# Strassen's seven products for half of a down projection, in a one-core transformer block in split float32

## What is computed

```python
m = rmsnorm(h, norm_mlp_g[l])
h = h + jnp.square(jax.nn.relu(m @ w_up[l])) @ w_down[l]      # w_up 2048 x 8192, w_down 8192 x 2048
return rmsnorm(h[:, CHUNK:CHUNK + S], final_norm_g)
```

## Time and profile before

| what | us |
|---|---|
| median of three runs (1141.16 to 1141.45) | 1141.17 |
| the profiled execution | 1139.69 |
| its span, first to last instruction | 1137.8 |
| TensorE busy | 1118.9 |
| VectorE busy | 714.9 |
| ScalarE busy | 605.3 |
| start of the first up stage, by the timeline | 415.8 |
| last matmul done | 1130.3 |

### The profile page before, as it was taken

One profiled execution on the slowest core, in us unless ns is written; L12 is line 12 of the kernel. 1 busy time (PEld: TensorE's weight loads), 2 busy tenths in 40 slices (PEclk: granted clock), 3 DMA queues, 4 the chain that ended last, 5 costly groups with the idle time before them and its releaser, 6 DMA issues.

```text
span 1137.8 us, 16740 instructions
## 1 busy us (share of the span) xinstructions
PE 1118.9 (98%) x6220; PEld 969.4 (85%) x6220; DVE 714.9 (63%) x986; ACT 605.3 (53%) x919; POOL 66.4 (6%) x78
## 2 busy tenths in 40 slices
PE   7999999999999999999999999999999999999997
PEld 7899999999878888888888888888888888888885
DVE  6986877777786666666664444446666665454453
ACT  8665666666665555555553333334555554344343
POOL 0001110111123320000000000000000000000000
PEclk9999999999999999999999999999999999999999
DMA  9544544334355545555555555555555555555541
GB/s 365 203 155 146 182 143 154 141 131 155 130 190 206 214 167 198 190 190 191 190 186 185 185 187 188 194 198 188 192 185 184 184 184 185 190 191 193 198 154 74
DMA packets 29573, 206.64 MB, mean 182 GB/s; under 512 B 3408, under 2 KB 3664, under 8 KB 5200
## 3 DMA queue, kind: packets, MB, share of 16 engines
q1 hardware_dynamic: 29232, 205.59, 50.8%
q10 hardware_dynamic: 288, 0.31, 0.1%
HBM read 203.79 MB, written 2.10 MB: 181 GB/s over the span
## 4 chain that ended last, share of the span: by engine, by line
PE 96%; ACT 1%; DVE 1%; DMA 1%; issue 0%; SPq 0%; POOL 0%; POOLq 0%; DVEq 0%
PE acc L329 58%; PE ps_qn L329 9%; PE ps_qr L329 9%; PE ps_v L329 8%; PE ps_kn L329 8%; PE ps_x L329 2%; DMA x_in<-x_all 1%; ACT hi L704 0%; PE ps_y L329 0%; ACT xs L742 0%; PE ps_qn L623 0%; PE ps_kn L494 0%; PE ps_y L522 0%; PE ps_qr L623 0%; SPq L271 0%
## 5 line engine op out<-in xcount | busy, mean ns | idle before, releaser
L1025 DVE TENSOR_TENSOR lo<-raw,hi 128x1024 fp32r<-128x1024 f32 (+1 forms) x379 | 462.6, 1221 | 290.7 <-ACT hi L704 286.6
L329 PE MATMUL acc<-xs,hi 128*128 128x512 f32 (+1 forms) x1952 | 586.3, 363 | 0.0
L704 ACT ACTIVATE hi<-raw 128x1024 fp32r<-128x1024 f32 (+1 forms) x379 | 397.8, 1050 | 293.2 <-PE ps_v L329 106.2
L329 PE MATMUL acc<-xs,lo 128*128 128x256 f32 (+1 forms) x1648 | 454.8, 284 | 7.2 <-DVE xs L1042 6.6
L329 PEld LDWEIGHTS acc<-xs,hi 128*128 128x128 f32 x1952 | 345.5, 189 | 51.9
L329 PEld LDWEIGHTS acc<-xs,lo 128*128 128x128 f32 x1648 | 311.7, 189 | 14.3 <-issue 6.6
L704 ACT ACTIVATE half_b<-acc 128x256 f32<-128x256 f32 x100 | 38.5, 385 | 155.0 <-PE acc L329 155.0
L329 PE MATMUL ps_v<-hi,hid 128*128 128x512 f32 x256 | 101.4, 396 | 0.0
L329 PE MATMUL ps_kn<-hi,hid 128*128 128x512 f32 x256 | 100.7, 393 | 0.0
L329 PE MATMUL ps_qr<-hi,hid 128*128 128x512 f32 x256 | 100.3, 396 | 0.0
L329 PE MATMUL ps_qn<-hi,hid 128*128 128x512 f32 x256 | 99.6, 393 | 0.0
(11 more groups left out here) (236 smaller groups left out, 942.1 us busy)
## 6 DMA issues: line engine op xcount, KB each, us to landing
raw<-w_up SPq DMA_DIRECT2D x64, 1024.0 KB, 4.7
raw<-w_down SPq DMA_DIRECT2D x64, 1024.0 KB, 4.7
raw<-w_in SPq DMA_DIRECT2D x42, 1024.0 KB, 4.7
raw<-w_o SPq DMA_DIRECT2D x16, 1024.0 KB, 4.8
h_res<-x_frames SPq DMA_DIRECT2D x1, 2048.0 KB, 7.6
x_in<-x_all SPq DMA_DIRECT2D x3, 544.0 KB, 7.5
consts<-consts_in SPq DMA_DIRECT2D x1, 1218.5 KB, 10.4
raw<-w_in SPq DMA_DIRECT2D x2, 512.0 KB, 8.6
```

Of the source, the lines that this page charges most:

```text
L329: return pe.matmul(o, l, m, start=start, stop=stop)
L704: return act.activation(o, i, ACT.Copy)
L1025: return dve.tensor_tensor(o, a, b, op)
```

## The change

**Seven products.** Half of the down projection (by hidden tiles) is computed in blocks of two by two: two hidden tiles a and b of 128 (a "pair"), two frame tiles, two column groups of 512. Eight block products become Strassen's seven (p1 to p7, in Winograd's form), each still of three matmuls of 512 columns. Each product sums over the pairs in its own bank: `p1 ps_qr, p2 ps_kn, p3 ps_v, p4 acc[1], p5 ps_x, p6 ps_qn, p7 acc[0]`; an eighth bank, `p8 ps_y`, takes one of the plain sums.

**Four segments.** The hidden columns go in 4 segments of 16 tiles: 16 up chunks, then 16 down chunks. Tiles 0 to 7 of a segment stay plain, tiles 8 to 15 form 4 pairs. Down chunks come in two sets of eight, one for each half of the output columns (a "mix"): pair 0, first 0, pair 1, second 0, pair 2, first 1, pair 3, second 1, where first and second are plain chunks of the left and the right column group, added into p2 and p4, and into p3 and p8. In the last segment the second set is 8 plain chunks with banks of their own. So there are 7 mixes and 28 pair chunks.

**On chip.** For a pair VectorE makes three mixed weights from raw (`t_31`, 1024 wide; `t_2`, 512, written over a quarter of raw; `t_4`, 512), ScalarE rounds them (`t_hi`, 1536 wide), VectorE makes `t_lo` (1536). In the up stage VectorE makes four mixed activations of 128 x 128 (`mixed_acts`), ScalarE rounds them (512 wide), VectorE makes their lo. After the last pair chunk of a mix ScalarE copies the product banks to SBUF (`read_out`: six, and p3 after the last plain chunk), VectorE adds p8 to `res`. The rest (`merge`, seven additions of 512 or 1024 elements per mix) is made by VectorE in the first eight up chunks of the next segment, or in the quad chunks at the end.

**Room.** Three raw buffers in the MLP in place of four (the fourth holds t_hi and a kept product); `gfin` is loaded in the last segment, into `xs`. The MLP's loops are written out.

```diff
+MIX = [("pair", 0), ("first", 0), ("pair", 1), ("second", 0), ("pair", 2), ("first", 1), ("pair", 3), ("second", 1)]
+TAIL_MIX = [("quad", q) for _ in range(2) for q in range(SEG // PER_CHUNK)]
...
+READ_ORDER = ("p2", "p6", "p1", "p7", "p5", "p4", "p3")
+STEPS = 7
...
             def load(src, c, more=0):
                 if c >= RAWS:
-                    sp.wait_ge(sem["lo_ready"], 2 * (c - RAWS) + 2 + 2 * more)
-                sp.dma_start(raw[c % RAWS][:], src).then_inc(raw_landed[c % RAWS], 16)
+                    before = c - (RAWS_MLP if c >= C_MLP + RAWS_MLP else RAWS)
+                    sp.wait_ge(sem["lo_ready"], 2 * before + 2 + 2 * more)
+                    if before in PAIR_OF:
+                        sp.wait_ge(sem["t_4"], PAIR_OF[before] + 1)
+                sp.dma_start(raw[raw_of(c)][:], src).then_inc(raw_landed[raw_of(c)], 16)
...
+            def product(o, x, w, first, last):
+
+                mm(o[:], x[0], w[0], first, False)
+                mm(o[:], x[0], w[1], False, False)
+                return mm(o[:], x[1], w[0], False, last)
...
+                pe.wait_ge(sem["lo_ready"], 2 * c + 1)
+                pe.wait_ge(sem["up_lo"], SEG * s + b + 1)
+                pe.wait_ge(sem["s_lo"], PAIRS * s + i + 1)
+                if first and mix:
+                    pe.wait_ge(sem["p_read"], STEPS * mix - 1)
+                product(prod["p2"], act_of(s, b, 0), unit(c, 0), first, last)
+                if first and mix:
+                    pe.wait_ge(sem["p_read"], STEPS * mix)
+                product(prod["p3"], mixed_act(3), unit(c, 1), first, False).then_inc(sem["chunk_used"], 1)
+                pe.wait_ge(sem["lo_ready"], 2 * c + 2)
+                product(prod["p6"], mixed_act(1), unit(c, 2), first, last)
+                product(prod["p1"], act_of(s, a, 0), unit(c, 3), first, last).then_inc(sem["chunk_used"], 1)
+                pe.wait_ge(sem["t_lo"], p + 1)
+                if first and g == 0:
+                    pe.wait_ge(sem["acc_read"], B_MLP + SEG * (s + 1))
+                product(prod["p7"], mixed_act(2), mixed_weight(0), first, last)
+                product(prod["p5"], mixed_act(0), mixed_weight(1), first, last)
+                product(prod["p4"], act_of(s, b, 1), mixed_weight(2), first, last).then_inc(sem["t_used"], 1)
...
                 act.wait_ge(sem["chunk_used"], 2 * (c - 2) + part + 1 + 2 * more)
+                if c in PAIR_OF and part == 1:
+                    act.wait_ge(sem["t_2"], PAIR_OF[c] + 1)
                 copy(halves(hi, c, part), raw_half(c, part)).then_inc(sem["hi_ready"], 1)
+                if c in PAIR_OF and part == 1:
+                    act.wait_ge(sem["t_4"], PAIR_OF[c] + 1)
+                    act.wait_ge(sem["t_used"], PAIR_OF[c])
+                    copy(t_hi[:], t_raw[:]).then_inc(sem["t_hi"], 1)
...
+                    split_hi(c + 2, 0)
+                    if d == 0:
+                        sums_hi(PAIRS * s + PAIRS - 1)
+                    if kind == "second" and n == QUADS - 1:
+                        act.wait_ge(sem["chunk_used"], 2 * c + 2)
+                        read_out(s, g, READ_ORDER[6:])
+                    split_hi(c + 2, 1)
+                    if kind == "pair" and n == PAIRS - 1:
+                        if s:
+                            act.wait_ge(sem["merged"], 2 * STEPS * s)
+                        act.wait_ge(sem["chunk_used"], 2 * c + 2)
+                        read_out(s, g, READ_ORDER[:3])
+                        act.wait_ge(sem["t_used"], PAIR_OF[c] + 1)
+                        read_out(s, g, READ_ORDER[3:6])
...
+                if p is not None and part == 0:
+                    dve.wait_ge(raw_landed[raw_of(c)], 16 * landings(c))
+                    if p:
+                        dve.wait_ge(sem["t_lo"], p)
+                    tt(t_of[:, 0:2, :], u[:, 1:3, :], u[:, 2:4, :], ALU.subtract).then_inc(sem["t_31"], 1)
+                    dve.wait_ge(sem["t_31"], p + 1)
+                    tt(u[:, 2, :], u[:, 1, :], t_of[:, 1, :], ALU.subtract).then_inc(sem["t_2"], 1)
+                if p is not None and part == 1:
+                    dve.wait_ge(sem["t_2"], p + 1)
+                    tt(t_of[:, 2, :], u[:, 0, :], u[:, 2, :], ALU.subtract).then_inc(sem["t_4"], 1)
                 dve.wait_ge(sem["hi_ready"], 2 * c + part + 1 + 2 * more)
                 tt(halves(lo, c, part), raw_half(c, part), halves(hi, c, part).bitcast(F32),
                    ALU.subtract).then_inc(sem["lo_ready"], 1)
+                if p is not None and part == 1:
+                    dve.wait_ge(sem["t_hi"], p + 1)
+                    tt(t_lo[:], t_raw[:], t_hi[:].bitcast(F32), ALU.subtract).then_inc(sem["t_lo"], 1)
...
+                    if j > PLAIN and j % 2:
+                        mixed_acts(PAIRS * s + pair)
+                    if s and j < PLAIN:
+                        for _ in range((2, 2, 1, 2, 2, 1, 2, 2)[j]):
+                            merge(merges)
+                            merges += 1
```

More of the change, by code:

```diff
@@ L304, in _ @@
                     load(w_o[4 * i + j], C_WO + j, 4 * i)
[L305 to L315, removed]
+            for s in range(SEGS):
+                c0 = C_MLP + s * C_SEG
+                for j in range(SEG):
+                    load(w_up[SEG * s + j], c0 + j)
+                for d in range(2 * HALF_D):
+                    load(w_down[2 * HALF_D * s + d], c0 + SEG + d)
+                    if s == SEGS - 1 and d == HALF_D:
+                        sp.wait_ge(sem["chunk_used"], 2 * (c0 + SEG))
+                        sp.dma_start(gfin[:], gfin_in).then_inc(sem["gfin"], 16)
             sp.wait_ge(sem["fin_act"], 1)
@@ new lines, in quad_chunk @@
+            def quad_chunk(s, c, q, banks, firsts, lasts):
+                for j in range(PER_CHUNK):
+                    if j % 2 == 0:
+                        pe.wait_ge(sem["lo_ready"], 2 * c + j // 2 + 1)
+                    for t in range(TILES):
+                        m = product(banks[t], act_of(s, PER_CHUNK * q + j, t), unit(c, j), firsts[t] and j == 0,
+                                    lasts[t] and j == PER_CHUNK - 1)
+                    if j % 2 == 1:
+                        m.then_inc(sem["chunk_used"], 1)
@@ L636, in m_parts @@
+            for s in range(SEGS):
+                c0, b0 = C_MLP + s * C_SEG, B_MLP + s * SEG
                 def m_parts(k):
                     pe.wait_ge(sem["m_lo"], k + 1)
[L639 to L665, removed]
@@ L682, in _ @@
[L682 to L698 removed]
+                if s:
+                    pe.wait_ge(sem["p_read"], STEPS * 2 * s - 1)
@@ new lines, in _ @@
+                for j in range(SEG):
+                    wide(c0 + j, b0 + j, x_wide, x_hi, ready=m_parts if s == 0 and j == 0 else None)
+                    if s == 0 and j == 0:
+                        turn(KT - 1)
+                        pe.wait_ge(sem["h_ss"], KT)
+                        mm(ps_x[:, 0:FRAMES], ones, sum_sq[:]).then_inc(sem["h_ss_ps"], 1)
+                cd = c0 + SEG
+                if s == 0:
+                    pe.wait_ge(sem["ht"], TILES * KT // 4)
+                    pe.wait_ge(sem["h_sd"], 1)
@@ new lines, in _ @@
+            for s in range(SEGS):
+                c0, b0, w0 = C_MLP + s * C_SEG, B_MLP + s * SEG, W_MLP + s * SEG
+                for j in range(SEG):
+                    n = SEG * s + j
+                    pair = (j - PLAIN) // 2
+                    acc_of[0] = acc[(b0 + j) % 2]
+                    split_hi(c0 + j + 2, 0)
+                    if j > PLAIN and j % 2 == 0:
+                        sums_hi(PAIRS * s + pair - 1)
+                    b_copy(c0 + j, w0 + j)
+                    split_hi(c0 + j + 2, 1)
+                    if s == 0 and j == 0:
@@ L1415, in up @@
+            merges = 0
+            for s in range(SEGS):
+                c0, b0, w0 = C_MLP + s * C_SEG, B_MLP + s * SEG, W_MLP + s * SEG
+                for j in range(SEG):
+                    n = SEG * s + j
+                    pair = (j - PLAIN) // 2
+                    split_lo(c0 + j + 2, 0)
+                    sum_ab(z[:], b0 + j, w0 + j).then_inc(sem["acc_read"], 1)
+                    if s == 0 and j == 0:
                         dve.wait_ge(sem["h_sd"], 1)
```

375 lines of the change are left out of this document (258 added, 117 removed).

## The result

| | before | after |
|---|---|---|
| median (runs) | 1141.16 us (1139.66 to 1141.45, 4) | 1121.87 us (1120.81 to 1123.17, 4) |
| the profiled execution | 1139.69 | 1123.17 |
| its span | 1137.8 | 1121.4 |

The ratio is 0.9836, 95% interval 0.9824 to 0.9848: 17.3 to 20.1 us faster. The forecast was 1127.5, the range 1122 to 1141; the median lies 0.13 us under its lower end, and the interval of the ratio, times 1141.16 (1121.1 to 1123.8 us), has that end inside it.

A forecast was written before the change was run, and what follows sets the result against it. TensorE, busy in nearly all of the MLP, was taken as the bound. Fewer matmuls -19.4, group changes +3.8 and up to down +2 gave -13.6 us: 1127.5 us from 1141.17, range 1122 to 1141.

The forecast's parts named there:

- What bounds the kernel: MLP: TensorE busy 714.45 of 714.5 us, so only fewer or cheaper matmuls shorten it, and gaps on TensorE add time.
- 84 matmuls, -19.4: Down stages: 28 pair chunks with 3 matmuls fewer each, at 0.2311 us a matmul, save 19.4 us.
- I keep 0.231 for them: Down stages: the matmuls left keep their 0.231 us rhythm, having the same width and operand kinds.
- The group changes, +3.8: First to second column group, three segments: TensorE waits for ScalarE's six reads, then p3's; 3 x 1.3 = 3.8 us.
- From up to down, +2: First two pairs of each segment: small margins before TensorE needs z and t_lo; 0.5 us charged four times.
- The margins of 0.1 and 0.2: Up to down: VectorE's z(15) ready 0.1 us before TensorE needs it, the second pair's t_lo 0.2 us before.
- Pair chunks and merges hidden: VectorE needs 9.2 us against TensorE's 10.40 per pair and plain chunk, 40.4 against 44.9 in eight up chunks with merges.
- three raw buffers and the code without loops: Put at zero: weight loads have 4.5 us spare; the down stages were already written out and showed no idle.
- The sum: Whole kernel: -19.4 + 3.8 + 2 = -13.6 us, giving a median of 1127.5 us.
- Nothing waits: Rival: VectorE's small operations cost less and all gaps close; 1121.8 us, chance 0.03.
- No head start: Rival: VectorE's new operations don't start before the one ahead ends; waits of 8 and 10 us, 1139.8 us, chance 0.12.
- VectorE is the bound: Rival: VectorE's run from up chunk 13 to the next group's t_4 is too slow; waits 25 us, 1147 us, chance 0.13.

The follow-up runs named there:

- e2: The kernel before with four segments of 16 up and 16 down chunks in place of two halves, all products plain: 1140.43 us, ratio 1.0003.
- e1: The kernel before with the MLP's activations in rows of 512 elements without the 16 meta columns, not 544: 1133.6 us, ratio 0.9942.
- e4: The changed kernel with ScalarE reading p3's bank before rounding the first half of the chunk after next, at a set's last plain chunk: 1120.49 us.
- e10: e4 with ScalarE reading three banks ahead of t_hi and VectorE making a segment's last z ahead of a lo: 1118.76 us, ratio 0.9804.
- e9: The changed kernel with each of the 49 merge additions cut to 8 elements into an unused place: 1121.13 us.
- e7: The kernel before with e1's layout and the up projection's input activations in rows of 512 elements: 1137.15 us, ratio 0.9965.
- e5: e4 with the MLP's input activations, the up projection's moving operand, in rows of 512 elements in place of 544: 1122.61 us.
- e8: The changed kernel with one more VectorE instruction per pair chunk ahead of t_4, a sum over 512 elements, 28 times: 1135.48 us.

## Why the prediction was right, point by point

- **What bounds the kernel**: right. Time left TensorE's down stages and nothing else; the up stages kept 89.7 for 16 chunks, the segments brought nothing (e2).
- **84 matmuls, -19.4**: the count is exact (6220 - 6136). At the rhythm that the changed kernel would have undisturbed, 0.2267, they are worth 19.0.
- **"I keep 0.231 for them"**: this step failed. The reason given, same width and operand kinds, was true and not enough, since the place of the stationary operand in memory changed with the new tiles. In the kernel before the same move is worth 6.8 us (e1: 355.0 to 348.2).
- **The group changes, +3.8**: right, 3 x 1.34 = 4.0 in the starts of the matmuls (2.5 of it shown as idle time). Both waits are the ones named: six reads behind a late t_hi, and p3 behind a hi (e4, e10).
- **From up to down, +2**: 1.1 (3 x 0.24 + 0.37). The chain of VectorE's starts held to 0.05 us. The margins of 0.1 and 0.2 were eaten by the hand-over to TensorE, for which no row stood: z(15) ends at 510.82, and the matmul that waited for it starts at 510.97. With z made earlier (e10) this first wait is gone in three segments. Why it is longer in the last segment is open.
- **Pair chunks and merges hidden**: right. t_hi took 1.49, t_lo 1.76 (predicted 1.50 and 1.76); merges hidden (e9). In the MLP no wait of TensorE ends in a load or in the loading of code, so three raw buffers and the code without loops cost nothing that shows.
- **The sum**. Measured in the MLP: -6.8 (layout) - 19.0 (products) + 5.1 (waits) + 2.1 = -18.6. The 2.1 is a term that the prediction didn't have, and the trace shows where it lies. In each pair chunk the nine matmuls whose weights are the mixed ones (`t_hi`, `t_lo`: p7, p5, p4) and the dozen behind them start 0.230 us apart on average (0.224 to 0.236) in place of 0.2267, also at pairs where TensorE doesn't wait; over 28 pair chunks these make 0.85 + 1.1 of the 2.1 us. `t_lo` lies at 320 bytes past a multiple of 512, `hi`, `lo` and `t_hi` at 128. Whether that is the cause, no run tests. The seven products alone, against a plain kernel with as good a layout, are worth 18.6 - 6.8 = 11.8 us (12.0 between e7 and e5): less than the forecast 13.6. So for the change that it described the forecast's gain was 1.8 too large. The 6.8 were missing from it; without them the median would be some 1128.7, next to the forecast's 1127.5, and it is they that carried the time to the very edge of the range. The errors point in opposite ways, but here the missing term made the forecast worse and not better: it was right on the waits and on what is hidden, and wrong on the rhythm.
- **The rivals**. *Nothing waits* named a number (1121.8) that was met almost exactly, and its cause is wrong: 5.1 us of waits are there, and the rest came from the layout. That the number was met is chance. *No head start* is out: VectorE's lo at 498.47 lasts to 499.70 and the next operation starts at 499.61, as before the change, and this one carries a wait. The section of the Trainium skill that the prediction read (VectorE: DVE Perf Modes, "The DRAIN you can't avoid") adds that a next operation that isn't held starts earlier. The prediction left that out, so its "the trace doesn't agree" is said of half the rule; the 0.09 us of this case does not speak against the whole of it. *VectorE is the bound* did not come about. e8 shows that its place was the right one: with 0.68 us more per pair 13.6 of the 19.3 us between the medians are gone.

## What to carry to other kernels

When tiles are placed anew, the rhythm of the matmuls that read them has to be measured anew. Here an offset of 32 to 128 bytes in the stationary operand was worth 4 to 6 us in 1120, and another row length with another offset 6.8, while the algorithm's saved products brought 19.0 before its waits and 11.8 behind them.

An engine with idle time on average can still be on the path. The margins at the changes of stage, worked out start by start from one profile, gave the waits of the group changes (1.3 predicted, 1.34 measured) and the effect of one more operation of 0.68 us (within 0.1 us at each place); only a clock that fell behind a long wait was not in them. And before an engine's work is cut, look at the order in which it does it: 3.8 us of the MLP came from putting a few instructions ahead of others.

## What the runs showed of the hardware that was not expected

- A 512-column float32r matmul with a weight load of 0.188 us beside it started every 0.2267 us or every 0.231 to 0.233 us, by where its stationary operand lay: fast with rows of 2048 bytes at 128 bytes past a multiple of 512, slow at 160, 192 and 256 past it, and in between (0.2311 on average, 0.226 to 0.236 in a pattern of 12) with rows of 2176 bytes. What the rule is, is open.
- The moving operand counts as well, in another sense: moving it from rows of 2176 to rows of 2048 bytes made an up chunk 0.047 us longer (90.45 against 89.70 for 16).
- Idle times of 2.2 us on TensorE were sometimes followed by 3.4 us at the lower clock level, which began only when TensorE was working again: at all three group changes of e8 (0.3 to 0.8 us behind the restart, 1.1 to 1.2 us lost each time), and behind the idle time that ends at 313 to 314 us in every trace in 5 of 14.
